# Expert up rows: four tokens' strips stacked in one gather, summed in column strips, gathered six turns later

## What is computed

```
for token t, head h:                       # 512 tokens, 8 heads
    experts[t,h,:], gates[t,h,:] = router  # 16 indices, softmax of 16 scores
    dots[s]  = down[experts[s]] . h_row[t]             s = 0..15
    coef[s]  = gelu(dots[s]) * gates[s]
    y[t]    += sum_s coef[s] * up[experts[s]]
out[t] = x[t] + gate2 * y[t]
```

## Time and profile before

| | us |
|---|---|
| median of 3 runs | 3002.66 (3001.5 to 3003.53) |
| the profiled execution, its own time | 2994.11 |
| its span (first to last instruction) | 2992.3 |
| PE busy in the span | 2625.3 (88%) |
| DVE busy | 1659.1 (55%) |
| POOL busy | 1169.9 (39%) |
| first gather issued | at 1497.4 |
| last gather issued | at 2975.8 |

### The profile page before, as it was taken

The page is one execution under the profiler, slowest core; times in us unless marked ns, Lnnn a source line. Parts: engine busy times, 40 slices in busy tenths (PEclk is TensorE's granted clock), DMA queues, the critical chain, the costliest instruction groups (busy, mean ns, idle before and its releaser), DMA issues.

```text
span 2992.3 us, 26054 instructions
## 1 busy us (share of the span) xinstructions
PE 2625.3 (88%) x8398; PEld 1372.6 (46%) x8398; DVE 1659.1 (55%) x3647; ACT 795.6 (27%) x1616; POOL 1169.9 (39%) x1091
## 2 busy tenths in 40 slices
PE   7999899999979979989799899979877778767777
PEld 3444444445544436467675465546422223223232
DVE  2056823345510124364379998765677777777764
ACT  2013312138730012232234323221312112212121
POOL 0000000013310000000057777656777777777776
PEclk8999999999989989999899899989999899989999
DMA  7226103122221113321379989999999999999998
GB/s 307 74 113 274 64 30 112 57 85 71 65 91 56 57 64 133 127 85 57 109 257 357 354 305 379 380 351 344 357 376 395 400 408 405 405 405 405 406 402 354
DMA packets 185462, 709.01 MB, mean 237 GB/s; under 512 B 20416, under 2 KB 43344, under 8 KB 175216
## 3 DMA queue, kind: packets, MB, share of 16 engines
q0 software_dynamic: 147456, 536.94, 46.7%
q1 hardware_dynamic: 37584, 169.45, 15.2%
q10 hardware_dynamic: 288, 0.96, 0.1%
HBM read 703.01 MB, written 4.27 MB: 236 GB/s over the span
## 4 chain that ended last, share of the span: by engine, by line
PE 22%; POOL 14%; issue 7%; DMA 5%; DVE 3%; ACT 0%; POOLq 0%; SPq 0%; DVEq 0%; ACTq 0%
PE bank L3193 14%; POOL ring L3001 11%; PE bank L488 4%; DMA ring<-in_peer_expert_down,experts 3%; POOL second_arena L3001 3%; DVE ring L3076 1%; PE bank L2035 0%; DMA second_arena<-in_peer_expert_down,experts 0%; DMA ring<-in_peer_expert_up,experts 0%; DMA x_rows_scratch<-second_arena 0%; DMA out<-xT 0%; PE bank L2012 0%; PE bank L2329 0%; PE bank L2336 0%; PE bank L2334 0%
## 5 line engine op out<-in xcount | busy, mean ns | idle before, releaser
L3193 PE MATMUL bank<-ring,xT 128*128 128x512 f32 x1516 | 765.6, 643 | 189.0 <-ACT xT L3169 81.4
L3076 DVE CUSTOM_DVE_ANT_0 ring<-ring,second_arena 128x1024 f32<-128x1024 f32 x380 | 465.9, 1226 | 219.8 <-DMA ring<-in_peer_expert_down,experts 172.4
L3193 PEld LDWEIGHTS bank<-ring,xT 128*128 128x128 f32 x1516 | 292.2, 203 | 600.4 <-issue 376.3
L3001 POOL DMA_INDIRECT ring<-in_peer_expert_up,experts x384 | 412.5, 1074 | 159.0 <-issue 96.7
L3001 POOL DMA_INDIRECT ring<-in_peer_expert_down,experts x380 | 402.4, 1059 | 131.3 <-issue 114.3
L488 PE MATMUL bank<-hT,ring 128*128 128x512 f32 (+2 forms) x1168 | 433.2, 530 | 6.4 <-DMA ring<-in_weights 1.8
L488 PEld LDWEIGHTS bank<-hT,ring 128*128 128x128 f32 (+1 forms) x1168 | 222.3, 193 | 211.0 <-issue 199.8
L1420 POOL TENSOR_TENSOR xs_skip<-xs_rows,rows 128x512 f32<-128x512 f32 x16 | 24.7, 1546 | 727.4 <-ACT xs_rows L1298 638.3
L3001 POOL DMA_INDIRECT second_arena<-in_peer_expert_down,experts x132 | 137.0, 1038 | 434.9 <-DVE experts L3059 390.6
L3169 ACT ACTIVATE xT<-consts,expert_coefs 128x128 f32<-128x128 f32 x505 | 177.9, 394 | 414.4 <-PE bank L3193 278.5
L3193 PE MATMUL bank<-second_arena,xT 128*128 128x512 f32 x504 | 239.2, 607 | 22.5 <-DMA second_arena<-in_peer_expert_up,experts 22.4
(11 more groups left out here) (527 smaller groups left out, 3107.7 us busy)
## 6 DMA issues: line engine op xcount, KB each, us to landing
ring<-in_weights SPq DMA_DIRECT2D x65, 2048.0 KB, 8.1
second_arena<-in_weights SPq DMA_DIRECT2D x12, 1024.0 KB, 8.2
decay<-acum_scratch SPq DMA_DIRECT2D x16, 512.0 KB, 5.2
ring<-in_peer_expert_up,experts POOLq DMA_INDIRECT x384, 7.3
ring<-in_peer_expert_down,experts POOLq DMA_INDIRECT x380, 7.1
second_arena<-in_peer_expert_down,experts POOLq DMA_INDIRECT x132, 6.5
x_rows<-in_x SPq DMA_DIRECT2D x1, 2048.0 KB, 12.0
x_rows_scratch<-second_arena SPq DMA_DIRECT2D x2, 1024.0 KB, 8.7
```

What stands on the lines that cost most here:

```text
L3001: pool.indirect_dma_start(out=slot[seat[n]], out_offset=None, in_=d[f"peer_expert_{kind}_2"], in_offset=bass.IndirectOffsetOnAxis(ap=exper ...
L3076: post(dve, dve.tensor_tensor_reduce(row, row, h_row(i), 1.0, 0.0, ALU.mult, ALU.add, dots[:, u % 2, s:s + 1]), dotted)
L3193: last = pe.matmul(k.bank[half][:], diag[n % DR], row[:, half * 512:(half + 1) * 512], start=(h == 0 and s == 0), stop=(h == RH - 1 and s ...
```

## The change

Four column strips. The coefficients and the experts of a unit are now stacked: ACT copies them (`stack`, 16 copies of 32 partitions x 4) so that up gather s = 4q + r of a unit brings, for the 32 tokens of strip r, four slots each: partition 32j + t' holds the expert of token 32r + t' in slot 4q + j. The matmul of such a gather has a stationary operand of 128 x 32 (four small diagonals under each other, made by ACT at line 3172 of the changed kernel) and writes 32 partitions of PSUM, strip r. A group of four gathers makes eight matmuls of 128x32 by 128x512, four strips for each half. PE waits for all four gathers of a group before its first matmul; each gather's buffer is released by its matmul in the second half.

Six turns later. The up row (u, s) is gathered in turn 16u + s + 6. PE runs late work to tick 16(u+1)+4q+8 before group q. There are 16 diagonal buffers in place of 8. `by_vector` and `sum_apart` are gone: PE sums all 512 gathers.

```
-    DR = 8
+    DR = 16
+    SW = 32
+    LAG = 6
...
-        for u in range(N):
-            for s in range(RK):
-                if u + 1 < N:
-                    order.append(("down", u + 1, s))
-                order.append(("up", u, s))
+        for n in range(RK * N + LAG):
+            if n < RK * (N - 1):
+                order.append(("down", n // RK + 1, n % RK))
+            if n >= LAG:
+                order.append(("up", (n - LAG) // RK, (n - LAG) % RK))
...
+                if kind == "up" and s == 0:
+                    pool.wait_ge(stacked.sem, u + 1)
...
+                which = experts[:, i, j:j + 1] if kind == "down" else t.up_rows[:, u % 4, s:s + 1]
...
-                dve.wait_ge(summed, (i + 1) * NSEL - (apart if i == NT - 1 else 0))
+                dve.wait_ge(summed, (i + 1) * NSEL)
...
+            def stack(out, rows):
+                out = out.rearrange("p (q s) -> p s q", s=4)
+                for s in range(4):
+                    for j in range(4):
+                        last = act.activation(out[j * SW:(j + 1) * SW, s, :], rows[s * SW:(s + 1) * SW, 4 * j:4 * j + 4],
+                                              ACT.Copy)
+                return last
...
+                act.wait_ge(routed.sem, u + 1)
+                if u >= 4:
+
+                    act.wait_ge(summed, (u - 3) * RK)
+                post(act, stack(t.up_rows[:, u % 4, :], experts[:, i, h * RK:(h + 1) * RK]), stacked)
...
+                post(act, stack(up_coef[:, u % 2, :], coef[:, u % 2, :]), k.astep)
...
-                        act.activation(diag[n % DR], k.const("ident"), ACT.Copy,
-                                       scale=coef[:, u % 2, s:s + 1]).then_inc(diag_ok.sem, 1)
...
+                    act.activation(diag[n % DR], strip_ident, ACT.Copy,
+                                   scale=up_coef[:, u % 2, s:s + 1]).then_inc(diag_ok.sem, 1)
...
-                for s in range(RK):
-                    other.upto(RK * (u + 1) + s + 2)
...
+                for q in range(RK // 4):
+                    n = RK * u + 4 * q
+                    other.upto(RK * (u + 1) + 4 * q + 2 + LAG)
...
+                    rows = [arrived(pe, ("up", u, 4 * q + s)) for s in range(4)]
+                    pe.wait_ge(diag_ok.sem, n + 4)
                     for half in range(2):
-                        last = pe.matmul(k.bank[half][:], diag[n % DR], row[:, half * 512:(half + 1) * 512],
-                                         start=(h == 0 and s == 0), stop=(h == RH - 1 and s == RK - 1))
-                    last.then_inc(summed, 1)
+                        for s in range(4):
+                            last = pe.matmul(k.bank[half][s * SW:(s + 1) * SW, :], diag[(n + s) % DR],
+                                             rows[s][:, half * 512:(half + 1) * 512],
+                                             start=(h == 0 and q == 0), stop=(h == RH - 1 and q == RK // 4 - 1))
+                            if half == 1:
+                                last.then_inc(summed, 1)
```

More of the change, by code:

```diff
@@ L2929, in expert_stage @@
         spent = k.xT[:, :, 0:H2]
-        diag = [spent[:, n // 2, (n % 2) * P:(n % 2 + 1) * P] for n in range(DR)]
+        diag = [spent[:, n // 8, (n % 8) * SW:(n % 8 + 1) * SW] for n in range(DR)]
+        up_coef = spent[:, 2, 0:2 * RK].rearrange("p (a s) -> p a s", a=2)
+        strip_ident = spent[:, 2, 64:64 + SW]
         x_back = spent[:, 4:8, :]
@@ L2942, in expert_stage @@
         weighed = Signal(ctx, nc, "expert_coefs_ready")
+        stacked = Signal(ctx, nc, "up_experts_stacked")
         diag_ok = Signal(ctx, nc, "coef_diagonal_ready")
@@ L2958, in scores @@
             return halves[i // HT].scores[i % HT]
-        def by_vector(u, s):
-            return u == N - 1 and s % 2 == 1 and s + 1 < RK
-        apart = sum(by_vector(N - 1, s) for s in range(RK))
-        extra = halves[1].scores[0][:, 0:D]
         def finish_tick(i):
@@ L3000, in _ @@
                 j = h * RK + s
+                which = experts[:, i, j:j + 1] if kind == "down" else t.up_rows[:, u % 4, s:s + 1]
                 pool.indirect_dma_start(
                     out=slot[seat[n]], out_offset=None, in_=d[f"peer_expert_{kind}_2"],
-                    in_offset=bass.IndirectOffsetOnAxis(ap=experts[:, i, j:j + 1], axis=0),
+                    in_offset=bass.IndirectOffsetOnAxis(ap=which, axis=0),
                 ).then_inc(here[seat[n]], 16)
@@ L3138, in _ @@
             weigh(N - 1)
-            sum_apart()
             finish(NT - 1)
@@ L3162, in _ @@
                 act.wait_ge(weighed.sem, u + 1)
+                if u == 0:
+                    for s in range(4):
+                        at = slice(s * SW, (s + 1) * SW)
+                        act.activation(strip_ident[at, :], k.const("ident")[at, at], ACT.Copy)
+                post(act, stack(up_coef[:, u % 2, :], coef[:, u % 2, :]), k.astep)
                 for s in range(RK):
                     n = diag_ok.n
-                    if not by_vector(u, s):
-                        if n >= DR:
-                            act.wait_ge(summed, n - DR + 1)
-                        act.activation(diag[n % DR], k.const("ident"), ACT.Copy,
-                                       scale=coef[:, u % 2, s:s + 1]).then_inc(diag_ok.sem, 1)
-                        diag_ok.n += 1
+                    if n >= DR:
+                        act.wait_ge(summed, n - DR + 1)
+                    act.activation(diag[n % DR], strip_ident, ACT.Copy,
+                                   scale=up_coef[:, u % 2, s:s + 1]).then_inc(diag_ok.sem, 1)
+                    diag_ok.n += 1
                     if s + 1 < RK:
@@ L3223, in second_block @@
         t.dots, t.coef = sb("expert_dots", [P, 2, RK]), sb("expert_coefs", [P, 2, RK])
+        t.up_rows = sb("stacked_experts", [P, 4, RK], I32)
         t.left = sb("scores_left_over", [P, RK * RK])
```

22 lines of the change are left out of this document (2 added, 20 removed).

## The result

The changed kernel takes **3015.8 us** (median of 20 runs, 2994.4 to 3033.2), beside 3001.2 us for the kernel before (20 runs, 2988.0 to 3012.4). The ratio is 1.0051, 95% interval 1.0034 to 1.0068: **slower by 15 us, where 16 us faster was forecast**, and just outside the range. The profiled execution took 3015.05 us with a span of 3013.0.

What follows compares the result with a forecast made beforehand. From 2200 us on POOL's issue and the DMA queues were taken as both full; only POOL's waits for PE in 1600 to 2200 us could shrink. Terms -28 + 8 + 4 = -16 us gave 2987 us, range 2955 to 3014.

Steps and rivals of the forecast that it cites:

- late work in pieces: Late stages: PE's late work in steps of four ticks, with new copies on ACT, costs 4 us (0 to 12).
- a wait in `finish(0)`: Border of two late stages: DVE waits for tile 0's last sum, moving store and late store; costs 8 us (5 to 13).
- Cheaper sums: 1600 to 2200 us: a group falls from 7.5 to 1.9 us on PE, so POOL waits less; gain 28 us (16 to 32).
- The fourth rival: Sums on PE: strips from different buffers don't run side by side, the gain is gone; 3050 us, chance 0.05.
- The long wait at the border: POOL's 13.7 us wait where two late stages meet behind a store; all of it hangs on `finish(0)`, which moves later.
- The step that failed: `finish` at tiles 1 and 2: DVE waits some 9 us, hidden with 1 us to spare; cost 0 (to 3).
- The second failed term: Unit borders: 16 copies each for coefficients and experts on ACT, 3.5 us a block; priced within 4 us (0 to 12).
- Groups hold buffers: Gathers-only stretch: each group holds its buffers until its fourth row; slack 1.1 us, where it was over 10; priced 0.
- the third rival: From 2200 us: buffers bind and POOL stops at every group of four; 3032 us, chance 0.17.
- Start and end: First gathers and last group: distances and number of gathers stay, last sums take about as long; 0, within 1 us.
- The first: Late stages: everything POOL waited for PE goes but the border; 40 us faster, 2963 us, chance 0.15.
- The second: A wash: late work in pieces and ACT blocks cost 12, the border 13, against 28 gained; about 3000 us, chance 0.20.

Runs made afterwards that it cites:

- no_lag_no_copies: The changed kernel with up rows in their old place (LAG = 0) and each block of 16 ACT copies made one; sums not the reference's: 2958.9 us, 0.9884.
- strips_no_lag: The changed kernel with LAG = 0 in place of 6, so up rows in their old place and strips kept: 2977.8 us, 0.9939 of the kernel before.
- finish_later: The changed kernel with finish(i) four dots later, after the dot of slot 7 in place of slot 3: 2994.1 us, 0.9975 of the kernel before.
- half_dots: The changed kernel with each DVE dot product over 512 of the 1024 columns, half left out: 2944.9 us, 0.9830 of the kernel before.

## Why the prediction was wrong, step by step

The runs make a chain from the kernel before to the changed one, each link but the first one edit, in us of 3001. By the intervals of the ratios the first step is known to 6 us, the others to some 10; the third is not clear of zero:

| link | ratio to before | step | the prediction |
|---|---|---|---|
| strips, no copies, no turns later (no_lag_no_copies) | 0.9884 | -35 | -28 (16 to 32) |
| the copies on ACT (strips_no_lag) | 0.9939 | +16.5 | +4 (0 to 12), with late work in pieces |
| six turns, without a wait in `finish` (finish_later) | 0.9975 | +11 | +8 (5 to 13), as a wait in `finish(0)` |
| `finish` where it was (the changed kernel) | 1.0051 | +23 | 0 (to 3) |

- **Cheaper sums.** The new group took what the rows said. PE runs 16 records of a warm group in 1.92 us (2001.74 to 2003.66) and of one at half clock in 3.64 (2639.62 to 2643.26):

```profile
2639.62 1.08 PE L3194 MATMUL bank<-ring,xT 128*32 128x512 f32 x3 [7.55 <-DMA second_arena<-in_peer_expert_up,stacked_experts]
...
2642.15 1.11 PE L3194 MATMUL bank<-ring,xT 128*32 128x512 f32 x3
2642.20 1.06 PE L3194 MATMUL bank<-second_arena,xT 128*32 128x512 f32 x1
```

  The fourth rival is out, and the drain of a switch is not to be seen: a group behind late work (2001.74, late work until 2001.81) took the same 1.92. The term was 28 and measured 35. The two traces say where, for gathers 32 to 399, which took 589.9 us before and 557.0 in no_lag_no_copies. POOL's waits for PE, less the ordinary 0.30 of each, gave 26.0 of these 33 us (54.1, then 28.1), less than the 31.8 that bounded them. Shorter gather instructions gave 10.4 (419.4, then 409.0), which the sum had at nothing; some 3 us of a wait for DVE go the other way. (The 61 short waits were not all 1.26 us at most: one was 1.86.)
- **The long wait at the border** is 16.7 us, before 13.7, and all its parts are where the prediction had them: `finish(0)` waits (6.88 us), the store, the late store, PE's wait (SPq, PE and POOL rows). From DVE's finish to POOL's next gather it took 31.3 us, before 34.1. The link's +11 has the size of the 8 forecast, but its uncertainty is as large as itself, and finish_later has the wait at the border no more and takes the same 580.6 us for gathers 32 to 399 as the changed kernel: that the size agrees is luck, the place was not where I had it. strips_no_lag took 568.6 there. Of the 12 us between, 11.0 are longer gather instructions (410.5, then 421.5) and 4.5 waits for PE, less 3.3 of a wait for DVE. What in the six turns makes them longer stays open.

```profile
1972.67 1.42 DVE L3100 TENSOR_TENSOR hT<-bank,gate 128x512 f32<-128x512 f32 x2 [6.88 <-PE bank L3194]
```
```profile
1975.43 0.62 SPq L3209 DMA_DIRECT2D out<-xT  x1
...
1982.68 0.44 SPq L2687 DMA_DIRECT2D x_rows_scratch<-second_arena  x1
```
```profile
1995.96 5.85 PE L488 MATMUL bank<-hT,second_arena 128*128 128x256 f32 x16 [23.46 <-SPq L1550]
2001.74 0.62 PE L3194 MATMUL bank<-second_arena,xT 128*32 128x512 f32 x1
```
```profile
2003.92 1.65 POOL L3003 DMA_INDIRECT second_arena<-in_peer_expert_up,stacked_experts  x1 [16.72 <-PE bank L3194]
```

- **The step that failed**: "At tiles 1 and 2 the same DVE wait is ... some 9 us ... Hidden, with 1 us to spare: 0 (to 3)." The wait was 9.08 and 9.09 us, and it was hidden in the sense meant: POOL did not wait for the buffer. But I asked only when buffers come free, and took POOL's instruction at 1.00 us whatever DVE did. The paragraph on what bounds the kernel even named the effect (POOL's instruction is longer while DVE is busy) and put it aside with "the change does not touch". The change does: a wait of DVE changes no work, but when it is done, from spread out to back to back. 23 us.
- **The second failed term**: the copies. 3.5 us a block was right (3.3 measured), but the spare time was read from ACT's busy share, which did not tell how much of an engine that works in order is free. 12 unit borders x 2 blocks x 3.3 us are 80 us of ACT's time; a fifth of it came through, nearly all as waits of POOL for PE (28.1 us without copies, 42.1 with them, for gathers 32 to 399). I took 4, the bound was 12, measured 14 to 16.5.
- **Groups hold buffers**: no wait over 0.3 us after 2200, landing 6.5 us (8.3 at most, where 8.9 was the bound) and groups at half clock of 3.6. Priced 0, right, and the third rival is out there. **Start and end**: the last finish starts 12.0 us behind the last gather, before 10.3 (2986.11 less 2975.81): 1.7 us, over the bound of 1.
- **The rivals.** The first is out: POOL's waits for PE did not go. The second, about 3000, came nearest with its time, and its copies are real, but the 23 us are in none of the four. The fourth's 3050 does not follow from the third's way of reckoning: 2.7 us short at each of 75 groups, a third of it absorbed, is some 135 us on top and not 50.
- **The execution itself.** The profiled execution reached its first gather 8.9 us later than that of before, through the same instructions. Over the traces of this study the first gather is at 1497 to 1501 us in the four kernels with full-width sums and at 1498 to 1508 in the ten with strips. The instructions up to it are the same and the two ranges overlap, so I give none of it to the change; the traces do not prove that.

The range was missed by 1.8 us only, and that is luck: the steps were off by -7, +12.5, +3 and +23, and partly cancel. It missed because two bounds were not bounds: each was worked out with one engine's cost fixed.

## What to carry to other kernels

When an engine is made to wait, ask not only who waits for it, but what its catching up runs against: work that is hidden when spread out can cost when it is done in one piece. Price the instruction that sets the rate, here POOL's gather, both with the other engine's work spread out and with it back to back. Put a wait for the last of a batch where the batch is done (here four dots later, 22 us), not where it stood before the order was shifted. Small instructions on an engine with a low busy share are not free if it works in order ahead of a critical one: 32 of 0.2 us per unit cost 15 us in all.

## What the runs showed of the hardware

A gather that POOL issues while a DVE instruction with two inputs of 128x1024 float32 runs is held until that instruction ends, and then takes 0.81 us: 58 of 58 gathers over 1.3 us in the changed kernel and 25 of 25 before, within 0.02 us. The other way round, in 2200 to 3000 us of the changed kernel 147 gathers begin in such an instruction with over 0.2 us of it left, and 145 of them are held; the other two begin 0.02 us behind its start. With dots of half the length the loss disappeared (half_dots). The Trainium skill, "SBUF — State Buffer", "Who interferes with whom", has the rule that a DVE instruction with two SBUF inputs contends with a GpSimd instruction that reads SBUF. Its section "SBUF: two separate sides" adds that whichever of the two starts first has the ports for its whole duration. The traces agree with the block (a gather reads its row numbers from SBUF). With "starts first" they agree when the dot is first, but for starts 0.02 us apart: the gather at 2351.13 us took 0.94 beside a dot that had begun at 2351.11, and it was that dot which took longer, 1.27 in place of 1.22. When the gather is first they do not agree: 260 dots and steps of `finish` begin while a gather runs, the nearest 0.03 us behind its start, and all 260 take their ordinary 1.22 or 1.23 us.

Four column strips of 128x32 by 128x512 took a quarter of four full-width sums (1.92 us against 7.5) with their rows in four different buffers, and at a granted clock of 0.50 they took 3.64 us. POOL did not wait for that; DVE did, in `finish`: the last group of tile 1 ran from 2337.29 to 2340.93 us, so 1.7 of DVE's 9.08 us are the half clock. Gathers of 128 rows of 4 KB ran at 1.30 us each where POOL needed only 1.27 (half_dots): 410 GB/s.
